# Delta-rule recurrence: one 128-column product for state and output of a head, bank sums by head parity, output factors on GpSimd

## What is computed

```python
def step(state, inp):
    r_t, w_t, k_t, v_t, a_t, b_t = inp
    sa = jnp.einsum('bhij,bhj->bhi', state, a_t)
    state = (state * w_t[:, :, None, :] + sa[..., None] * b_t[:, :, None, :]
             + v_t[..., None] * k_t[:, :, None, :])
    return state, jnp.einsum('bhij,bhj->bhi', state, r_t)
...
y = ((y - mean) * lax.rsqrt(var + RW_LN_EPS)).reshape(bsz, t_len, RW_WIDTH)
y = (y * ln_g + ln_b).astype(h.dtype)
bonus = jnp.sum(rh * kh * r_k, axis=-1, keepdims=True) * vh
o_rw = (y + bonus.reshape(bsz, t_len, RW_WIDTH)) * g
```

## Time and profile before

| | us |
|---|---|
| median of 3 runs | 1509.59 (1509.31 to 1510.66) |
| profiled execution | 1508.68 |
| its span | 1506.9 |
| PE busy | 1276.4 (85%) |
| DVE / ACT / POOL busy | 450.9 / 274.4 / 270.6 |
| DMA, mean over the span | 329 GB/s, 496.40 MB |

### The profile page before, as it was taken

How to read it: one execution, slowest core, us unless ns; L and a number is a source line. 1 busy time by engine, 2 the same in 40 slices (tenths; PEclk the granted TensorE clock), 3 DMA queues, 4 the chain that set the end, 5 groups by cost and what they waited for, 6 DMA issues and landing times. The chain is left out here.

```text
span 1506.9 us, 21513 instructions
## 1 busy us (share of the span) xinstructions
PE 1276.4 (85%) x9120; PEld 689.4 (46%) x9120; DVE 450.9 (30%) x893; ACT 274.4 (18%) x543; POOL 270.6 (18%) x163
## 2 busy tenths in 40 slices
PE   9999999999998999767667667999998776676577
PEld 5755466546877544223223323856544322232232
DVE  2554653645746521101000101295411010010011
ACT  2142400323422222100000000115211110011010
POOL 0676226742022009920000000000000000000000
PEclk9999999999999999888888999999999888899889
DMA  9932363236631899999999999946899999999997
GB/s 371 366 136 84 145 246 112 112 112 260 261 141 38 337 388 408 431 432 432 434 431 432 431 432 423 395 169 244 338 435 428 432 431 431 431 432 431 432 433 315
DMA packets 34066, 496.40 MB, mean 329 GB/s; under 512 B 5456, under 2 KB 8400, under 8 KB 11728
## 3 DMA queue, kind: packets, MB, share of 16 engines
q1 hardware_dynamic: 34000, 495.45, 79.1%
HBM read 493.34 MB, written 2.10 MB: 329 GB/s over the span
## 5 line engine op out<-in xcount | busy, mean ns | idle before, releaser
L3341 PE MATMUL banks<-weight_ring,spare_weights_arena 128*32 128x512 f32 x1472 | 207.3, 713 | 131.2 <-DMA weight_ring<-in_moe_weights 129.3
L3233 DVE TENSOR_TENSOR spare_weights_arena<-spare_weights_arena,banks 64x512 f32<-64x512 f32 x32 | 22.1, 691 | 652.9 <-ACT spare_weights_arena L3142 652.9
L3341 PEld LDWEIGHTS banks<-weight_ring,spare_weights_arena 128*32 128x32 f32 x1472 | 53.0, 127 | 277.1 <-issue 212.1
L3285 PE MATMUL banks<-spare_weights_arena,x 128*128 128x64 f32 x960 | 110.5, 273 | 0.0
L3285 PEld LDWEIGHTS banks<-spare_weights_arena,x 128*128 128x128 f32 x960 | 109.6, 192 | 0.0
L3142 ACT ACTIVATE spare_weights_arena<-banks 64x512 f32<-64x512 f32 x32 | 18.9, 591 | 484.1 <-PE banks L3341 484.1
L3359 PE MATMUL banks<-weight_ring,spare_weights_arena 128*32 128x512 f32 x688 | 87.8, 654 | 12.3 <-issue 7.6
L1005 POOL TENSOR_TENSOR weight_ring<-spare_weights_arena,weight_ring 128x2048 f32<-128x2048 f32 x16 | 74.0, 4636 | 70.8 <-DVE spare_weights_arena L849 38.5
L1118 PE MATMUL banks<-weight_ring,x_normed_hT_mix 128*128 128x512 f32 x192 | 84.7, 592 | 0.0
L3411 PE MATMUL banks<-spare_weights_arena 64*128 64x512 f32 x240 | 59.6, 614 | 20.9 <-ACT spare_weights_arena L3150 20.9
L3341 PE MATMUL banks<-x_normed_hT_mix,spare_weights_arena 128*32 128x512 f32 x272 | 41.4, 759 | 31.4 <-DMA x_normed_hT_mix<-in_moe_weights 31.4
(11 more groups left out here) (557 smaller groups left out, 1796.3 us busy)
## 6 DMA issues: line engine op xcount, KB each, us to landing
weight_ring<-in_moe_weights SPq DMA_DIRECT2D x52, 4096.0 KB, 25.1
weight_ring<-in_ring_weights SPq DMA_DIRECT2D x35, 2048.0 KB, 12.3
weight_ring<-in_moe_weights SPq DMA_DIRECT2D x28, 2048.0 KB, 11.9
spare_weights_arena<-in_moe_weights SPq DMA_DIRECT2D x13, 4096.0 KB, 54.0
x_normed_hT_mix<-in_moe_weights SPq DMA_DIRECT2D x6, 4096.0 KB, 52.1
spare_weights_arena<-in_moe_weights SPq DMA_DIRECT2D x8, 2048.0 KB, 12.3
weight_ring<-in_moe_weights SPq DMA_DIRECT2D x10, 1024.0 KB, 6.6
x_normed_hT_mix<-in_moe_weights SPq DMA_DIRECT2D x8, 1024.0 KB, 7.0
```

The costliest lines, as they stand in the source:

```text
L3233: dve.tensor_tensor(hid[0:2 * CAP, :], sil[0:2 * CAP, :], b_gu[2 * CAP:4 * CAP, :], ALU.mult).then_inc(s_h, 1)
L3285: ins = pe.matmul((b_x, b_dn)[k // 4][:, k % 4 * 2 * CAP:(k % 4 + 1) * 2 * CAP], g.x[:, tt, k * P:(k + 1) * P], Pr[:, tt, :], start=(tt == ...
L3341: ins = pe.matmul(b_gu[q:q + CAP, :], xg[:, 2 * quarter + k, e * CAP:(e + 1) * CAP], up_w(where, quarter, k)[:, which, e, :], start=(quart ...
```

## The change

- `Ark`'s masked blocks and k lie side by side in `of_kr`, AB's left block and b in `of_br`: for each head 128 columns, which give the chunk's increment of the state on one half of the partitions and its output on the other. GH keeps its 128 columns for both.
- `of_values` is one product of 128 columns per head for state and output, and GH times X likewise; both add up in the pair of banks `PAIR[c]`, one bank per parity. The products of r and the state, and the old state itself (a product with the identity), are added there by PE. DVE's adds for X, for the state and in `normed` go away; X's start value `Aak` times v is computed chunk by chunk into the banks of X.
- ACT copies X's even heads and y, DVE X's odd heads; the state is decayed one parity at a time.
- c1 and gn are computed by GpSimd after the last T_step (s_dT 10), into the place of `lora_g2`.
- masks j = 6 and 7 wait for two transposes; k's and a's transposes change places; PE waits for its own r products (s_rS).

```diff
-    L, a, kk = tiles(), tiles(), tiles()
-    q1 = g.take(1024)
+    L, kk = tiles(), tiles()
+    a_q1 = g.take(2 * 4 * S)
+    a = a_q1[:, 0:4 * S].rearrange("p (a t) -> p a t", a=4)
...
-    Aab, Aak, Ark = blocks(flat(L)), blocks(flat(E)), blocks(q1)
-    AB = xs_flat.rearrange("p (q a i n) -> p q a i n", q=2, a=TT, i=4)
+    Aab, Aak = blocks(flat(L)), blocks(flat(E))
+    four = lambda ap: ap.rearrange("p (a i x t) -> p a i x t", a=TT, i=4, x=4)
+    of_kr, of_br = four(a_q1), four(xs_flat)
+    both = lambda ap, h: ap[:, h // 2, 2 * (h % 2):2 * (h % 2) + 2, :].rearrange("p x t -> p (x t)")
...
-    AkV = flat(a).rearrange("p (a n) -> p a n", a=TT)
+    AkV = g.mixn[0:64, 0, 0:HALF]
...
-    c1 = flat(E).rearrange("p (a n) -> p a n", a=TT)
+    c1 = lora_g2.rearrange("p (a n) -> p a n", a=TT)
...
+    PAIR = (6, 2, 4, 6)
+    y_of = lambda c, q: byp(y[:, (c // 2) * HALF:(c // 2 + 1) * HALF])[low[c % 2], :, q, :]
+    y_bank = lambda c, q: of_bank(PAIR[c] + q)[low[1 - q], 0:4, :]
...
+        pool.wait_ge(s_vc, TT)
+        pool.wait_ge(s_boc, 1)
+        pool.wait_ge(s_par, 48)
+        pool.wait_ge(s_dT, 10)
+        link = g.pool_steps.link
+        for tt in range(TT):
+            link(pool, pool.tensor_tensor(h8(c1[:, tt, :]), h8(vn[:, tt, :]), b8(bonus, tt), ALU.mult))
+            link(pool, pool.tensor_tensor(c1[:, tt, :], c1[:, tt, :], lnb, ALU.add))
+            link(pool, pool.tensor_tensor(c1[:, tt, :], c1[:, tt, :], gn[:, tt, :], ALU.mult))
+            pool.tensor_tensor(gn[:, tt, :], gn[:, tt, :], lng, ALU.mult).then_inc(s_c1, 1)
...
-            act.copy(knat[:, tt, :], ps[4 + tt]).then_inc(s_kc, 1)
+            act.copy(of_br[:, tt, :, 0:4:3, :], ps[4 + tt].rearrange("p (i q t) -> p i q t", i=4, q=2)).then_inc(s_kc, 1)
         for tt in range(TT):
             act.wait_ge(s_kt, 2 + tt + 1)
-            act.copy(AB[:, :, tt, :, 64:128], ps[6 + tt].rearrange("p (i q t) -> p q i t", i=4, q=2)).then_inc(s_kc, 1)
+            act.copy(of_kr[:, tt, :, 0:4:3, :], ps[6 + tt].rearrange("p (i q t) -> p i q t", i=4, q=2)).then_inc(s_kc, 1)
...
+        def y_out(c, q):
+            act.wait_ge(s_dS, 2 * c + q + 1)
+            act.copy(y_of(c, q), y_bank(c, q)).then_inc(s_ye, 1)
...
+        def x_copy(c):
+            q0 = 64 * (c % 2)
+            act.wait_ge(s_X, 2 * c - 1)
+            act.copy(byp(X)[q0:q0 + 64, :, 0, :], of_bank(0)[q0:q0 + 64, 0:4, :]).then_inc(s_Xc, 1)
+        for c in range(1, 4):
+            x_copy(c)
+            for q in range(2):
+                y_out(c - 1, q)
+        y_out(3, 0)
...
+            if j < 4:
+                dst = (Aab, Aak)[j // 2][:, q].rearrange("p a i t -> p (a i) t")
+            else:
+                dst = (of_br, of_kr)[j // 2 - 2][:, :, :, 1 + q, :]
                 src = src.rearrange("p (a i) t -> p a i t", a=TT)
                 mk = con["le"].unsqueeze(1).unsqueeze(1).to_broadcast([P, TT, 4, 64])
+            if j == 6:
+                dve.wait_ge(s_kt, 2)
...
-        dve.wait_ge(s_vc, TT)
-        dve.wait_ge(s_boc, 1)
-        dve.wait_ge(s_par, 48)
-        b8 = lambda col, tt: col[:, 8 * tt:8 * tt + 8].unsqueeze(2).to_broadcast([P, 8, 64])
-        h8 = lambda ap: ap.rearrange("p (h e) -> p h e", e=64)
-        dve.wait_ge(s_AV, TT)
-        for tt in range(TT):
-            link(dve, TT_(h8(c1[:, tt, :]), h8(vn[:, tt, :]), b8(bonus, tt), ALU.mult))
-            link(dve, TT_(c1[:, tt, :], c1[:, tt, :], lnb, ALU.add))
-            mark(TT_(c1[:, tt, :], c1[:, tt, :], gn[:, tt, :], ALU.mult))
-            mark(TT_(gn[:, tt, :], gn[:, tt, :], lng, ALU.mult))
...
-            dve.wait_ge(s_ye, tt + 1)
-            dve.wait_ge(s_rS, 3)
-            lo = 64 if tt == 0 else 0
-            for q in range(2):
-                yv = byp(yt)[lo:P, :, q, :]
-                ins = TT_(yv, yv, of_bank(4 + q)[lo:P, 4 * tt:4 * tt + 4, :], ALU.add)
-                if q == 0:
-                    mark(ins)
-                else:
-                    ins.then_inc(s_yr, 1)
-            g.dve_steps.wait(dve)
-            dve.wait_ge(s_yr, tt + 1)
+            dve.wait_ge(s_ye, (4, 7)[tt])
+            if tt == 1:
+                dve.wait_ge(s_yr, 1)
...
+            dve.wait_ge(s_c1, tt + 1)
...
-                dve.wait_ge(s_X, c)
-                for q in range(2):
-                    TT_(byp(X)[q0:q0 + 64, :, q, :], of_bank(q)[q0:q0 + 64, 0:4, :],
-                        byp(AkV[:, c // 2, :])[q0:q0 + 64, :, q, :], ALU.add).then_inc(s_Xc, 1)
+                dve.wait_ge(s_X, 2 * c)
+                dve.tensor_copy(byp(X)[q0:q0 + 64, :, 1, :], of_bank(1)[q0:q0 + 64, 0:4, :]).then_inc(s_Xd, 1)
             if c == 3:
                 break
-            dve.wait_ge(s_dS, c + 1)
-            fresh = ps[3 - c % 2][:, 0:256].rearrange("p (a i) -> p a i", a=4)
-            if c == 0:
-                TT_(St[1], fresh, dec(0), ALU.mult).then_inc(s_S, 1)
-            else:
-                link(dve, TT_(Ssum, fresh, St[c % 2], ALU.add))
-                TT_(St[(c + 1) % 2], Ssum, dec(c), ALU.mult).then_inc(s_S, 1)
-            dve.wait_ge(s_S, c + 1)
+            for q in range(2):
+                dve.wait_ge(s_dS, 2 * c + q + 1)
+                TT_(St[(c + 1) % 2][low[q]], of_bank(PAIR[c] + q)[low[q], 0:4, :], dec(c)[low[q]], ALU.mult).then_inc(s_S, 1)
...
-        for out, left in ((4, Aak), (6, Ark)):
-            for tt in range(TT):
-                for h in range(8):
-                    for c2 in range(2):
-                        hs = slice(h * 64, (h + 1) * 64)
-                        ins = pe.matmul(ps[out + tt][rows[c2], hs], left[rows[c2], h % 2, tt, h // 2, :],
-                                        vn[rows[c2], tt, hs], start=(out == 4 or h == 0), stop=(out == 4))
-                if out == 4:
-                    ins.then_inc(s_AV, 1)
+        hs = [slice(h * 64, (h + 1) * 64) for h in range(8)]
+        of_head = lambda h: slice((h // 2) * 64, (h // 2 + 1) * 64)
+        def of_values(c):
+            t, tt = rows[c % 2], c // 2
+            for h in range(8):
+                ins = pe.matmul(ps[PAIR[c] + h % 2][:, of_head(h)], both(of_kr[t, tt], h), vn[t, tt, hs[h]],
+                                start=(h < 2), stop=False, skip_group_check=True)
+            ins.then_inc(s_V, 1)
+        for h in range(8):
+            ins = pe.matmul(ps[4][rows[0], hs[h]], Aak[rows[0], h % 2, 0, h // 2, :], vn[rows[0], 0, hs[h]], start=True, stop=True)
+        ins.then_inc(s_AV, 1)
+        of_values(0)
...
-                                        AB[rows[c2], q, tt, i, :], start=True, stop=True)
+                                        both(of_br[rows[c2], tt], 2 * i + q), start=True, stop=True)
...
-        state_at = lambda c, h: ps[3 - c % 2][rows[h % 2], (h // 2) * 64:(h // 2 + 1) * 64]
-        x_of = lambda c, h: (X[rows[c % 2], hs[h]] if c else AkV[rows[0], 0, hs[h]])
-
-        def of_values(c, h):
-
-            t = rows[c % 2]
-            pe.matmul(state_at(c, h), knat[t, c // 2, hs[h]], vn[t, c // 2, hs[h]], start=(h < 2), stop=False)
-
-        for h in range(8):
-            of_values(0, h)
+        x_of = lambda c, h: (X[rows[c % 2], hs[h]] if c else AkV[:, hs[h]])
+        x_at = lambda c, h: ps[h % 2][rows[c % 2], of_head(h)]
         pe.wait_ge(s_GHc, 1)
         for c in range(4):
             t, tt = rows[c % 2], c // 2
             tk = slice(c * CH, (c + 1) * CH)
-            if c == 1:
+            if c:
+                pe.wait_ge(s_XV, c)
+                for q in range(2):
+                    pe.wait_ge(s_S, 2 * (c - 1) + q + 1)
+                    for n in range(4):
+                        ins = pe.matmul(x_at(c, 2 * n + q), kk[rows[q], n, tk], St[c % 2][rows[q], n, :], start=False, stop=(n == 3),
+                                        skip_group_check=True)
+                    ins.then_inc(s_X, 1)
+                pe.wait_ge(s_V, c + 1)
+                for q in range(2):
+                    for n in range(4):
+                        ins = pe.matmul(ps[PAIR[c] + q][rows[1 - q], of_head(2 * n)], r[rows[q], n, tk], St[c % 2][rows[q], n, :],
+                                        start=False, stop=False, skip_group_check=True)
+                    if c < 3:
+                        ins = pe.matmul(ps[PAIR[c] + q][rows[q], 0:256], ident[rows[q], rows[q]],
+                                        St[c % 2][rows[q]].rearrange("p a i -> p (a i)"), start=False, stop=False,
+                                        skip_group_check=True)
+                ins.then_inc(s_rS, 1)
+                pe.wait_ge(s_rS, c)
+            for q in range(2):
+                if c:
+                    pe.wait_ge((s_Xc, s_Xd)[q], c)
+                for n in range(4):
+                    ins = pe.matmul(ps[PAIR[c] + q][:, of_head(2 * n)], GH[t, q, tt, n, :],
+                                    x_of(c, 2 * n + q), start=False, stop=(n == 3), skip_group_check=True)
+                ins.then_inc(s_dS, 1)
+            if c == 0:
```

(30 more changed lines are left out.)

37 lines of the change are left out of this document (15 added, 22 removed).

## The result

The changed kernel takes 1534.34 us (median of 4 runs, 1532.57 to 1536.88) against 1509.45 (4 runs, 1508.36 to 1510.66): a ratio of 1.0166, 95% interval 1.0147 to 1.0184. Its profiled execution took 1535.62 us for a span of 1533.8. The forecast was 1520.1, its range 1512.5 to 1524.0: slower as foretold, but by 24.9 us and not by 10.5.

The account below looks back on a forecast made before the run. PE's instruction order was taken to bound the changed recurrence, whose end shifts the remainder: 12.5 us longer there, less 1.95 gained ahead, net 10.5 us slower, 1520.1 us; range 1512.5 to 1524.0.

Parts of the forecast that it names:

- The clock is full ... and nothing in the change makes PE idle longer: In the stretches priced, PE's granted clock is 1.00 (2.4 GHz) and stays there, so full-clock paces apply.
- The new form's pace: PE's products with 128 stationary columns: 0.110 us per instruction, bounds 0.058 and 0.115.
- L: Rival: stationary width is free, all products pace at 0.058 us; +3.8 us, 1513.4 us; chance 0.11.
- F: Rival: fewer instructions, each at the alternating pace of 0.031 us; -3.8 us, 1505.8 us; chance 0.05.
- kk, r, the identity products and the wait for s_rS: First part of a middle chunk in PE's order: 0.93, 0.93, 0.46 and 0.44 us, one after the other.
- Joint product, values' and change of form: Next part of a middle chunk in PE's order: 1.76, 1.76 and 0.15 us.
- Middle chunk: Chunk 1 or 2 of the recurrence, bound by PE's order: 7.36 us against 3.27 before the change.
- Ahead of the recurrence: Four changes before or at the recurrence's start: gains of 1.04, 0.50, 0 and 0.41 us, together 1.95.
- R: Rival: loads and products in one row half don't overlap, 0.058 us more per instruction; +16.7, 1536.8 us; chance 0.01.
- S: Rival: the later stream of weights, bound by its own volume, swallows the delay; 1509.6 us; chance 0.05.
- In the new recurrence VectorE reads banks, so 0: GpSimd's factors beside the recurrence slow no VectorE step there: 0 us; they run hidden for 13 to 14 us.
- One for one: A shift of the recurrence's end shifts the whole remainder equally, since the later DMA issues wait for PE's chain.

Follow-up runs that it names:

- with all rows: Changed kernel with all 128 rows in each joint product of 128 stationary columns, same instruction count and order, computing other sums: 1519.18 us, ratio 1.0066.
- with the other half filled: Changed kernel with an unread product of constants beside each 128-column product, in the array's other row half: 1520.43 us, ratio 1.0071.
- the stream: Kernel before with 128 products of constants, 64 rows by 64 stationary columns in one quadrant, put ahead of the recurrence: 1524.20 us.
- the streams: Kernel before with constant products ahead of the recurrence, five variants of rows, stationary and moving columns: 1524.79, 1536.30, 1524.20, 1524.14 and 1535.32 us.
- factors later: Kernel before with the four output factors per half on GpSimd, started only behind VectorE's last SBUF-only step in the recurrence: 1510.21 us, ratio 0.9998.

## Why the prediction missed

**The step that failed** is the sentence "The clock is full ... and nothing in the change makes PE idle longer". Its premise, that only idle time could cost the clock, was never in the rows: they showed full clock for before's mix of products, not for a long run of 64 rows by 128 columns with 64 moving columns, of which the rows have five instructions. In its place the runs showed a clock that falls to 0.50 under such a run with PE busy throughout, and with it a middle chunk of 11.36 us, where it took 6.77 with all rows and a clock of 1.00. The Trainium skill ("TensorE: Matmul & The Clock Gate", Part 1) says that the gate goes by how busy the engine has been; busy in the sense of the profile's column disagrees, with 11.25 of 11.36 us busy at 0.50. The profile's busy time does not show how much of the array works.

**The size of it.** At full clock the forecast holds: 1520.1 foretold; 1519.18 with all rows and 1520.43 with the other half filled. The changed kernel's 1534.34 is 15.2 us above the run with all rows. In the two traces: the recurrence is 33.67 - 21.90 = 11.8 us longer, 24 instructions of the output product behind it take 12.81 us against 10.52, 2.3 more, and it starts 1.1 us later (477.53 against 476.40). The first two, 14.1 us, are the clock, and by an estimate it cost some 1.2 us more, since at full clock three pairs of products would each be 0.4 us shorter than with all rows (3.32 against 3.72). Of the later start 0.5 us is there at L1858 (420.79 against 420.26 us), ahead of the first changed instruction. The profiled spans differ by 16.7; of that 1.5 us lie further on, and I did not trace them.

**Term by term**, from the timeline with all rows:
- The new form's pace: taken at 0.110, 0.115 measured ((2.00 - 0.27)/15 for 16 instructions at 449.11 us in the changed kernel). Near right; L the rival is refuted (0.058), and F with it.
- kk, r, the identity products and the wait for s_rS: 2.76 foretold, 489.95 - 488.09 = 1.86 measured. Two quadrants' runs overlap where one ends and the next begins, and r's last products run beside the identity's. I had counted all as one after the other.
- Joint product, values' and change of form: 3.67 foretold, 493.67 - 489.95 = 3.72; with 64 rows, 3.32, since their ends overlap, which the sum left out.
- `Aak` times values: 0.93 foretold, 1.20 to the next kk.
- Middle chunk 7.36 foretold, 6.77 measured; chunk 0 4.60 and 481.32 - 476.40 = 4.92; chunk 3 3.84 and 3.43. Sum 23.16 and 21.90, 1.26 less.
- Ahead of the recurrence: a gain of 1.95 foretold, but with all rows L2030 starts at 476.40 us and not at 475.70. Of these 0.70 us, 0.38 are there at L1858 (420.26 us, against 419.88 for the same product in before), ahead of the first changed instruction. In the changed kernel L1931's replacement measured a gain of 0.88 (1.04 foretold), and two pauses of PE with no releaser in the trace (0.63 and 0.85 us) took back what the rest gave. These two misses, a recurrence 1.26 us too long and a start 0.70 us too early, partly cancel; that the sum at full clock came out within 1 us owes something to it.

**The rivals.** R, loads and products that don't overlap, gave 1536.8 us, nearest to the result, for a reason that is wrong: at full clock one quadrant still paces at 0.058 (256 instructions in 15.04 us in the stream) and the new form at 0.115. A time that agrees proves no mechanism. S is refuted by the streams.

**GpSimd.** "In the new recurrence VectorE reads banks, so 0" is right for the changed kernel, whose profile shows L1788, a reader of banks, at 0.42 and 0.43 us beside GpSimd (478.67 and 479.56 us). In the old recurrence the same move costs about 4 us: L1727's 1.77 us was the sign of it, and L1785, SBUF alone, was the step to look at. The eight operations were put at 13 to 14 us, from L1525's 1.6 for one; they took 10.1, since those 1.6 were measured beside L1727, and the other L1525 of before have half of 2.5.

**One for one** held: 22.9 us at the end of the recurrence, 24.9 at the end of the kernel, with 2 us of slow output products between.

## What to carry to other kernels

Before a product is made wider to save instructions, ask how much of the array it puts to work and for how long: 64 rows by 128 columns took 0.115 us for each instruction, two of 64 columns in turn 0.06, and a run of the wide ones cost the clock in a kernel whose PE was 99% busy. Read the granted clock of the stretch that you change, and price the edit at both levels where its mix of products is new to the kernel. A step moved to GpSimd stretches VectorE's operations on two SBUF operands beside it, and is free only where these have time to spare; and a pause of 1 us in a recurrence of small products can cost some 3 more behind it.

## What the runs showed of the hardware

- The granted clock fell under an engine that the profile shows as 100% busy: half the rows with 64 moving columns, or all rows with 32, lost it; half the rows with 128 moving columns, all rows with 64, and one quadrant at twice the pace held it. Adding work in the idle row half made a kernel 14 us faster; adding it in the busy half made it 26 us slower.
- The price of an f32 instruction with 128 stationary columns is 0.11 us at full clock with 2, 64 and 128 moving columns, and with 64 rows as with 128: 16 of them in 1.84 us, 128 in 14.51 and in 14.55.
- The pause of 1.02 us in before's recurrence was followed by 0.50; the pauses of 0.45 us that it always had the earlier trace rows were not.
- Beside GpSimd, VectorE's operations with both operands in SBUF took 1.39 us instead of 0.43 and 1.64 instead of 0.69; those that read a bank kept to 0.42 and 0.43, and a reduction with one operand (L1763 at 491.56 us, factors later) to 0.69.
